# An expert layer whose weights are loaded in longer runs into ten joined slots

## What is computed

```python
def _hier_moe(x, w_coarse, b_coarse, w_fine, b_fine, w_gate, w_up, w_down):
    ...
    gate = jnp.zeros((n, N_EXPERTS), f32).at[jnp.arange(n)[:, None], eidx].add(wt)
    hg = jnp.einsum('nd,edf->nef', xs, w_gate)
    hu = jnp.einsum('nd,edf->nef', xs, w_up)
    act = jax.nn.silu(hg) * hu * gate.astype(x.dtype)[:, :, None]
    out = jnp.einsum('nef,efd->nd', act, w_down)
```

## Time and profile before

| what | value |
|---|---|
| median of 3 runs | 1838.98 us (1836.88 to 1843.45) |
| the profiled execution's own time | 1840.96 us |
| its span | 1838.9 us |
| TensorE busy, share of the span | 1486.7 us, 81% |
| VectorE, ScalarE, GpSimd busy | 566.0, 285.2, 296.1 us |
| mean rate of all transfers over the span | 275 GB/s |
| mean granted clock of TensorE | 0.912 of full |

### The profile page before, as it was taken

The page is one execution under the profiler, slowest core; times in us unless marked ns, Lnnn a source line. Parts: engine busy times, 40 slices in busy tenths (PEclk is TensorE's granted clock), DMA queues, the critical chain, the costliest instruction groups (busy, mean ns, idle before and its releaser), DMA issues.

```text
span 1838.9 us, 19426 instructions
## 1 busy us (share of the span) xinstructions
PE 1486.7 (81%) x7565; PEld 839.3 (46%) x7565; DVE 566.0 (31%) x1407; ACT 285.2 (16%) x565; POOL 296.1 (16%) x402
## 2 busy tenths in 40 slices
PE   6899999798989996878787788788787787777870
PEld 5677776577758773433233233233233232233330
DVE  2779999666651223101010010010010010010015
ACT  2111111333320001111111011011011011011111
POOL 0066665333200000000000000000000000000006
PEclk9899999999979997988988998888999998899895
DMA  9324242335317625999999999999999999999964
GB/s 284 117 92 138 92 138 92 116 118 163 108 29 230 229 92 193 395 398 393 378 382 369 377 384 387 381 376 372 383 370 373 380 378 376 372 387 390 367 241 151
DMA packets 253055, 505.27 MB, mean 275 GB/s; under 512 B 23572, under 2 KB 99556, under 8 KB 233708
## 3 DMA queue, kind: packets, MB, share of 16 engines
q1 hardware_dynamic: 235788, 493.74, 74.5%
q0 software_dynamic: 5200, 9.19, 1.6%
q10 hardware_dynamic: 12016, 1.66, 0.6%
HBM read 503.18 MB, written 26.28 MB: 288 GB/s over the span
## 4 chain that ended last, share of the span: by engine, by line
DMA 35%; PE 26%; SPq 6%; DVE 1%; POOL 1%; issue 1%; ACT 0%; POOLq 0%; ACTq 0%; DVEq 0%
DMA ring<-in_w_up_dram 34%; PE bank L1261 16%; SPq L384 6%; PE bank L1191 6%; PE bank L1282 1%; PE bank L900 1%; DMA ring<-expert_rows 0%; PE bank L1158 0%; PE bank L1141 0%; POOL arena L862 0%; POOL arena L863 0%; PE bank L1169 0%; DVE arena L1798 0%; PE bank L1211 0%; PE bank L1228 0%
## 5 line engine op out<-in xcount | busy, mean ns | idle before, releaser
L1261 PE MATMUL bank<-ring,arena 128*64 128x512 f32 x2048 | 518.8, 664 | 156.8 <-DMA ring<-in_w_up_dram 156.8
L1261 PEld LDWEIGHTS bank<-ring,arena 128*64 128x64 f32 x2048 | 196.4, 152 | 452.6 <-issue 452.6
L1282 PE MATMUL bank<-ring,arena 128*64 128x512 f32 x1024 | 259.8, 666 | 19.0 <-DVE arena L1785 19.0
L1780 DVE SCALAR_TENSOR_TENSOR arena<-arena,gcol 64x512 f32<-64x512 f32 x32 | 23.8, 743 | 728.8 <-ACT arena L727 728.8
L930 PE MATMUL bank<-arena,ring 128*128 128x280 f32 x768 | 188.8, 405 | 3.0 <-ACT arena L579 1.9
L930 PEld LDWEIGHTS bank<-arena,ring 128*128 128x128 f32 x768 | 145.9, 192 | 44.1 <-issue 7.6
L1282 PEld LDWEIGHTS bank<-ring,arena 128*64 128x64 f32 x1024 | 80.5, 152 | 174.6 <-issue 174.6
L839 POOL DMA_INDIRECT expert_rows<-arena,idx_dst x32 | 29.5, 922 | 800.2 <-ACT arena L732 800.2
L732 ACT ACTIVATE arena<-bank 64x512 f32<-64x512 f32 x128 | 75.9, 593 | 330.0 <-PE bank L1282 328.8
L1191 PE MATMUL bank<-ring,arena 128*128 128x256 f32 x512 | 114.8, 386 | 0.0
L1228 PE MATMUL bank<-ident,arena 64*128 64x64 f32 x721 | 66.3, 239 | 56.7 <-DVE arena L1780 47.5
(11 more groups left out here) (333 smaller groups left out, 1403.9 us busy)
## 6 DMA issues: line engine op xcount, KB each, us to landing
ring<-in_w_down_dram SPq DMA_DIRECT2D x64, 2048.0 KB, 21.2
ring<-in_w_gate_dram SPq DMA_DIRECT2D x64, 2048.0 KB, 19.6
ring<-in_w_up_dram SPq DMA_DIRECT2D x64, 2048.0 KB, 22.6
ring<-in_w_in_dram SPq DMA_DIRECT2D x20, 2048.0 KB, 8.7
ring<-in_w_out_dram SPq DMA_DIRECT2D x8, 2048.0 KB, 9.7
ring<-in_s_w_glu_dram SPq DMA_DIRECT2D x2, 2048.0 KB, 8.4
arena<-v_samples SPq DMA_DIRECT2D x8, 512.0 KB, 4.4
ring<-expert_rows SPq DMA_DIRECT2D x4, 1024.0 KB, 9.3
```

The source lines that it names most:

```text
L1261: ins = pe.matmul(PB[b][at:at + CAP, :], xgT[b][:, kk, :], slot(s, KD // 2)[:, k, :], start=(kk == 0), stop=(kk == KD - 1))
L1282: ins = pe.matmul(PB[2 + cc // 2][at:at + CAP, :], hT[:, f, :], slot(4 + half, KF // 2)[:, k, cc * 512:(cc + 1) * 512], start=(f == 0), st ...
```

## The change

The expert stage has ten slots in place of six. Four new ones lie in the arena (`tab_slots`, which are slots 6 and 7, and `x1_slots`, which are 8 and 9), over buffers that the first part or the routing has finished with. Experts with an even number take slots 6, 7, 4, 5 for gate and up, those with an odd number take 0, 1, 8, 9, and the down halves of all take 2 and 3. So gate and up of an expert are loaded into slots that the expert two before it has left. Down halves still wait for the expert just before.

In a slot, partition p now holds rows p*8 to p*8+7 of a gate or up half (one run of 16 KB in DRAM) and rows p*2 and p*2+1 of a down half (also one run of 16 KB). For that the order of the contraction changes: `transpose_rows` picks every eighth number of a gathered row, and the activations are turned by every second one. The gain of the norm is loaded once more in that order (`ffn_gain`).

The gathered rows and the results of even and odd experts now share one buffer each, in partitions 0 to 63 and 64 to 127. The rows of `x1` are overwritten by slots 8 and 9, so they come back from DRAM (`x1_end`) near the end, with the final gain. ScalarE's squares go to PSUM. Gather and scatter keep their places in GpSimd's stream. The core of the diff:

```diff
@@ slots
-        FILLS = [len(range(s, NPRE, PRE_SLOTS)) for s in range(4)] + [0, 0]
-        MOE_SLOT = (2, 3, 0, 1)
+        FILLS = [len(range(s, NPRE, PRE_SLOTS)) for s in range(4)] + [0] * 6
+
+        slots = [ring[:, i, :] for i in range(6)] + tab_slots + x1_slots
+        GATE_UP = ((6, 7, 4, 5), (0, 1, 8, 9))
+        DOWN = (2, 3)
@@ SyncE
-                sp.dma_start(slot(MOE_SLOT[q], KD // 2), src.rearrange("a (k p) n -> p (a k) n", p=P)) \
-                    .then_inc(slot_loaded[MOE_SLOT[q]], 16)
+                sp.dma_start(slot(s, KD // 2), src.rearrange("a (p k) n -> p (a k) n", p=P)) \
+                    .then_inc(slot_loaded[s], 16)
...
+                sp.dma_start(ffn_gain[:, :, :], t["norm_ffn"][0].rearrange("(h p k) -> p h k", h=2, p=P)).then_inc(gain_loaded, 16)
...
+            sp.wait_ge(os_done, NS)
+            for b in range(3):
+                sp.wait_ge(S0_stored[b], 16 * len(range(b, NS, 3)))
             for b in range(2):
-                sp.wait_ge(S0_stored[b], 16 * len(range(b, NS, 3)))
-            for s in (4, 5):
-                load_down(0, s)
+                sp.wait_ge(st_stored[b], 16 * NH // 2)
             for q in range(4):
-                sp.wait_ge(out_done, 2 * (NO - 3 + q))
-                load_gate_up(0, q)
+                load_gate_up(0, 0, q)
+            for n in range(OUT_AT + 4, NPRE):
+                pre_load(n)
+            for h in range(2):
+                sp.wait_ge(out_done, 2 * (NO - 3 + h))
+                load_down(0, h)
+            sp.wait_ge(out_done, 2 * (NO - 1))
+            load_gate_up(1, 1, 0)
...
+            def round_loads(R):
+
+                def down(x, e):
+                    for h in range(2):
+                        sp.wait_ge(down_done, x * 2 + (h - 1))
+                        load_down(e, h)
+
+                if is_first(R):
+                    down(1, 1)
+                with sp.Fori(1 if is_first(R) else 0, NE // 2) as i:
+                    for b in range(2):
+                        x = i * 2 + (R * NE + b)
+                        for q in range(4):
+                            sp.wait_ge(gate_up_done, x * 2 + (q // 2 - 3))
+                            load_gate_up(i * 2 + b, b, q)
+                        down(x, i * 2 + b)
+
+            extra = run_rounds(sp, round_loads)
+
+            sp.wait_ge(gate_up_done, extra * (2 * NE) + (2 * NE - 2))
+            for tile in TILE_ORDER:
+                sp.dma_start(x1_end[0:TT[tile], tile, :], x1_dram[tile * P:tile * P + TT[tile], :]).then_inc(x1_back[tile], 16)
@@ TensorE
-                    ins = turn_64(PB[4 + k // 8][:, (k % 8) * CAP:(k % 8 + 1) * CAP], xg[p][0:CAP, k * P:(k + 1) * P], k == 0)
+                    half, kk = divmod(k, KD // 2)
+                    rows = xg[p][:, half * (D // 2):(half + 1) * (D // 2)].rearrange("t (p k) -> t k p", k=KD // 2)[:, kk, :]
+                    ins = turn_64(PB[4 + half][:, kk * CAP:(kk + 1) * CAP], rows, k == 0, p)
```

## The result

| | before | after |
|---|---|---|
| median of 4 runs each, us | 1839.9 (1836.9 to 1843.5) | 1860.4 (1853.7 to 1861.6) |
| ratio, 95% interval | | 1.0106 [1.009, 1.0122] |
| profiled execution, span, us | 1838.9 | 1851.6 |

The change makes the kernel slower by 20.5 us, 1.1%. The profiled execution of after is the shortest of its four, 1853.68 us; against its counterpart it shows 12.7 of the 20 us.

A forecast was written before the change was run, and what follows sets the result against it. Loads bound the kernel; after the change scatter and gather would, at 29.2 + 2.6 + 2.9 = 34.7 us a period. That gave +27.1 and +1.3 for the edges: 1840.96 + 28.4 = 1869.4, or 1867 as a median, range 1780 to 1905.

The forecast's parts named there:

- the chain of scatter and gather: Expert stage, from one down projection through scatter, gather, transposes and copy to the next: 29.2 us before what lengthens it.
- What bounds now, and what next: Expert stage: weight loads bound the 33.7 us period now; after the change scatter and gather decide.
- Loads alone, 31.1 us: Expert stage: period that loads with 16 KB packets would allow, 28.9 us of transfer plus 2.2 us kept.
- Turns, +1.5 and +1.1 us: Transfer engines: waiting turns behind longer packets adds 1.5 us to the scatter and 1.1 to the gather, +2.6 together.
- The chain's sum, 34.7 us: Expert stage period with scatter and gather deciding: 29.2 + 2.6 + 2.9 us, bounds 30.7 and 37.7.
- The clock, +2.9 us: TensorE after a pause of 8 us: low clock adds 1.2 us to transposes and 1.7 to the down projection.
- Strided transposes, nothing: Transposes reading gathered rows with a step of eight: nothing taken for the sum, at most 2.2 us a period.
- Edges, +1.3 us: Before and after the expert stage: +1 for expert 1's loads during the first gather, +0.3 for the gain's load.
- (2): Expert stage: packet length does not reach scatter and gather; period 32.1 us, 48 us won, 1791; chance 0.27.
- (3): Expert stage: loads decide at 31.1 us a period; 78 us won, 1761; chance 0.07.
- (4): Expert stage: the two effects cancel, period within 0.2 us of now, 1834 to 1844; chance 0.13.
- (5): Expert stage: strided transposes cost 2.2 us on top, period 36.9 us, 1933; chance 0.08.

The follow-up runs named there:

- the edit of GpSimd's order: GpSimd issues the next gather before it waits for the scatter's landing: 1784.7 us on the changed kernel, 1843.4 us on the kernel before.
- the run of the 26 matmuls: The changed kernel with 26 extra matmuls per expert between the end of gate and up and the wait for the gathered rows: 2301.5 us, ratio 1.2506.

## Why the prediction was right, and where its steps were off

The mechanism held: the chain of scatter and gather decides, lengthened by the packets and by the clock. That direction and size came out too, 1867 forecast and 1860.4 measured, is in part luck: an error of 0.9 us a period in the sum pushed the same way as what the sum left out. By its own steps:

- *What bounds now, and what next.* The loads bound the kernel before, and the chain was "only a little behind". Shown by the edit of GpSimd's order, nothing before the change and 76 us after it. With landings as short as before, a chain that decides takes 31.8 us (six slots, 8 KB), so it was some 2 us behind. The forecast signs came: TensorE waits for the rows in all 32 experts, never for up, SyncE waits at the down halves (975 us in 62 times), and the DMA share is 0.94.
- *Loads alone, 31.1 us.* Measured 31.7 to 31.8 where loads decide, 0.6 us more. What of it is packets and what the losses beside them is not shown; but 8 KB runs end at 31.8 too, so the 0.5 us that the line from 428 to 436 GB/s promised did not come.
- *Turns, +1.5 and +1.1 us.* Measured +1.2 for the scatter (9.1 against 7.9) and +1.3 for the gather: 2.5 in all for 2.6. That this fits so well is partly luck. By the line through the two packet sizes each landing should grow by 1.5 us from 8 to 16 KB; the pairs of runs give 1.5 (ten slots) and 1.7 (six) for both together. The rest came from the slots, for which the sum had no term, and with six slots the scatter does not grow at 16 KB at all. It takes long packets and ten slots. What differs is when SyncE issues the next gate and up: with ten slots 0.9 to 2.4 us after D, ahead of the scatter, with six 7.4 and 14.2 us after. While a scatter was under way the engines moved 422 and 426 GB/s with ten slots, 401 and 373 with six. That fewer loads stand beside the scatter's last turns would fit; no run isolates it, so it stays an inference.
- *The chain's sum, 34.7 us.* Here is the step that was off. The gather's landing is counted from the start of its issue (1306.71 to 1315.08 is 8.37), so the gather's own 0.9 us was in it already and I added it again. Counted once, the sum is 33.8 us and the forecast 1840, no change: that it said "slower" rests on this error. Measured was more than 33.8: 34.1 us over the 30 periods that it stands for (the last took the 31.1 us that it was given), 10 us in all; the rest of the way from 1840 to 1860.4 is mostly the 6.7 us by which the median lies above the profiled execution, and 1.5 us at the edges. From D(0) to D(31) the forecast was 1072.1 us and 1055.0 were measured, 17.1 less: 27 from the 0.9 us, and some 10 back, mostly from the down projections (next point). With the edges the profiled execution is 15.7 us under the sum's 1869.4; the median of the runs is 6.6 us under the forecast.
- *The clock, +2.9 us.* From the rows to the down projection 3.8 us were measured in the expert of the chain above for the 3.6 taken, and 9.1 us of down for the 8.8. The size was right, the reason only half. The pause does cost the clock: filling most of it is worth 1.8 us a period where the transposes have no step. But in the change the stepped read and the low clock cover the same time; with the pause nearly filled the transposes still take 2.9 us and down still 9.1, and the median gains only 10.6 us.
- *Strided transposes, nothing.* Right for this kernel (0.1 us a period by the run without the step), and only because the clock is low. They are worth 48.6 us once the pause is mostly filled, a part of it through the down projection, which the prediction did not tie to them.
- *Edges, +1.3 us.* D(0) is 2.8 us later.
- *The rivals.* (2) decides "from a growth of under 1.6 us in the two landings together"; they grew by 2.5. (3), the loads, is what decides with the chain out of the way, at 1784.7 and not at 1761. (4) ended at 1844; the median is 16 us above it, some 0.5 us a period. (5) needed 2.2 us a period from the step; the run without it gives 0.1.

Two small versions beat both kernels at 1785: six slots with runs of 8 KB, and long runs with the gather ahead of the wait. They don't add up, since at 31.7 to 31.8 us the loads decide.

## What to carry to other kernels

When two things arrive together, making one faster shows only what the other allows: work out the second chain's length before speeding up the first. Longer packets can make the bulk stream faster and the small transfers beside it slower, so try the length in steps; here 8 KB gave 54 us with six slots, 16 KB took back 46 of them, and with ten slots all of them and 20 us more. Count a latency from the event from which the profile counts it, or a step's own time comes in twice.

## What was not expected of the hardware

- Transposes whose operand is read with a step (17 records of rows with a step of eight, 5 of activations with a step of two) take 132 ns each in place of 81 at granted clock 1.00, and 143 in place of 138 at 0.50. With the rows in partitions 64 to 127 it is 115 in place of 72, and 126 in place of 121. The 2.52 us stand in the run of the 26 matmuls too, in a window where the share of the DMA engines is 0.00.
- A matmul of 512 f32 columns to 64 rows of a bank is two records of 432 ns when all go to the same half, 222 to 224 ns a record when they take turns on two halves.
- With GpSimd's order changed, scatter and gather are in flight together, and the gather lands in 11.4 us in place of 8.8 (the scatter in 8.3 in place of 8.0, ten slots and 16 KB); the period still falls by 2.4 us.
- After stepped transposes the down projection ran in part or wholly at the lower clock in most experts: in 30 of 32 where TensorE had paused for 1.7 us before them, and in 22 of 32 where it had not paused at all.
